# Regrouping value steps and maxima tiles on TensorE in a two-layer hybrid attention kernel

## The reference

```
s = einsum('bqkgd,blkd->bkgql', qblk, k) * scale      # scores
p = softmax(s, axis=-1)                               # over context + latent keys
o = einsum('bkgql,blkd->bqkgd', p, v)                 # value step
```

## Time and profile before

| what | us |
|---|---|
| median of 3 runs | 1099.52 (1099.34 to 1104.13) |
| profiled execution's own time | 1105.77 |
| its span, first to last instruction | 1103.9 |
| PE busy | 969.0 |
| DVE busy | 594.0 |
| attention, first layer | about 255 to 520 |
| attention, last layer | about 811 to 1030 |

### The profile page before, as it was taken

The page is one execution under the profiler, slowest core; times in us unless marked ns, Lnnn a source line. Parts: engine busy times, 40 slices in busy tenths (PEclk is TensorE's granted clock), DMA queues, the critical chain, the costliest instruction groups (busy, mean ns, idle before and its releaser), DMA issues.

```text
span 1103.9 us, 13093 instructions
## 1 busy us (share of the span) xinstructions
PE 969.0 (88%) x4607; PEld 684.6 (62%) x4607; DVE 594.0 (54%) x901; ACT 403.4 (37%) x815; POOL 524.8 (48%) x421
## 2 busy tenths in 40 slices
PE   4799999996899899998995299899968999999793
PEld 2478777985554455555784289789755445555572
DVE  5419230244568499824069548341645758782337
ACT  1521122314354466554200333133434445555320
POOL 2227232352557455553345337243626756566464
PEclk9799999996899899999998689899959989899997
DMA  9756451215232100012431022123142130001421
GB/s 364 270 178 218 157 188 40 77 31 125 55 77 65 34 16 8 16 58 79 169 96 77 38 62 72 58 65 85 49 101 65 37 72 16 15 16 58 160 69 77
DMA packets 44976, 96.91 MB, mean 88 GB/s; under 512 B 9592, under 2 KB 16656, under 8 KB 42864
## 3 DMA queue, kind: packets, MB, share of 16 engines
q1 hardware_dynamic: 43472, 90.83, 26.8%
q10 hardware_dynamic: 1440, 5.24, 1.2%
HBM read 71.33 MB, written 5.26 MB: 69 GB/s over the span
## 4 chain that ended last, share of the span: by engine, by line
PE 71%; DVE 10%; POOL 4%; ACT 4%; SPq 4%; DMA 3%; issue 3%; POOLq 0%; ACTq 0%; DVEq 0%
PE banks L762 13%; PE banks L764 12%; PE banks L763 12%; PE banks L936 11%; PE banks L956 9%; PE banks L914 5%; SPq L588 3%; PE banks L773 2%; DMA area_g<-in_w_ada_dram 2%; DVE negmax L1635 1%; PE banks L975 1%; DVE stats L1515 1%; DVE area_b L1779 1%; PE banks L968 1%; PE banks L826 1%
## 5 line engine op out<-in xcount | busy, mean ns | idle before, releaser
L1393 POOL TENSOR_TENSOR w_split<-w_raw,w_split 128x512 fp32r<-128x512 f32 (+4 forms) x124 | 146.2, 1184 | 258.7 <-ACT w_split L1138 258.6
L762 PE MATMUL banks<-w_split,area_a 128*128 128x512 f32 (+3 forms) x624 | 232.7, 373 | 16.4 <-DVE area_a L1845 9.9
L764 PE MATMUL banks<-w_split,area_a 128*128 128x512 f32 (+3 forms) x624 | 229.8, 368 | 0.0
L763 PE MATMUL banks<-w_split,area_a 128*128 128x512 f32 (+3 forms) x624 | 229.7, 368 | 0.0
L1635 DVE TENSOR_REDUCE negmax<-banks 128x1 f32<-128x768 f32 x160 | 149.6, 951 | 67.3 <-PE banks L914 66.4
L1138 ACT ACTIVATE w_split<-w_raw 128x512 fp32r<-128x512 f32 (+4 forms) x124 | 69.9, 581 | 278.1 <-PE banks L764 278.1
L936 PE MATMUL banks<-area_a 97*128 97x512 f32 (+4 forms) x448 | 135.7, 416 | 17.5 <-DMA area_a<-m_row 11.5
L762 PEld LDWEIGHTS banks<-w_split,area_a 128*128 128x128 f32 x624 | 119.4, 191 | 46.2 <-issue 16.4
L1237 ACT ACTIVATE area_z<-banks 128x512 f32<-128x512 f32 x196 | 109.1, 595 | 103.5 <-PE banks L936 98.2
L764 PEld LDWEIGHTS banks<-w_split,area_a 128*128 128x128 f32 x624 | 118.9, 190 | 16.6
L763 PEld LDWEIGHTS banks<-w_split,area_a 128*128 128x128 f32 x624 | 119.2, 191 | 15.5
(11 more groups left out here) (184 smaller groups left out, 1458.4 us busy)
## 6 DMA issues: line engine op xcount, KB each, us to landing
area_g<-in_w_ada_dram SPq DMA_DIRECT2D x16, 1024.0 KB, 5.8
w_raw<-in_w_in_dram SPq DMA_DIRECT2D x32, 512.0 KB, 3.7
area_g<-in_w_ada_dram SPq DMA_DIRECT2D x16, 512.0 KB, 5.0
w_raw<-in_w_out_dram SPq DMA_DIRECT2D x16, 512.0 KB, 3.9
area_a<-parts SPq DMA_DIRECT2D x72, 96.0 KB
area_a<-parts SPq DMA_DIRECT2D x30, 192.0 KB, 3.6
area_b<-in_x_dram SPq DMA_DIRECT2D x8, 512.0 KB, 9.8
x_mid<-area_b ACTq DMA_DIRECT2D x6, 512.0 KB, 2.7
```

The lines of the kernel that those rows point to most:

```text
L762: nc.tensor.matmul(dst, a[0], b[0], start=first, stop=False)
L763: nc.tensor.matmul(dst, a[0], b[1], start=False, stop=False)
L764: return nc.tensor.matmul(dst, a[1], b[0], start=False, stop=last)
L1393: op = nc.gpsimd.tensor_tensor(lo, raw, hi.bitcast(F32), ALU.subtract)
```

## The change

In each iteration p = 1 to 9 of both layers, two value steps are moved next to each other twice. `mix(L, p, 0)` goes behind tile 1 and `turn_max`, directly ahead of `mix(L, p, 1)`. Tile 4 goes behind `mix(L, p, 3)`, and the second `mla_head` goes ahead of `mix(L, p, 2)`. The lists of the other engines are not touched, and no instruction is added or removed. In iteration 8 and 9 there are no tiles of pair p+2, and in iteration 9 no `turn_max` either.

```
@@ -1042,9 +1042,9 @@
                     max_tile(L, p + 2, 0)
                     turn_denominators(L, p - 1)
                     turn_output(L, p - 1)
-                    mix(L, p, 0)
                     max_tile(L, p + 2, 1)
                     turn_max(L, p + 1)
+                    mix(L, p, 0)
                     mix(L, p, 1)
                     if head_pair(p + 3):
                         mla_head(L, 2 * p + 6)
@@ -1052,11 +1052,11 @@
                     max_tile(L, p + 2, 2)
                     scores(L, p, 5)
                     max_tile(L, p + 2, 3)
-                    mix(L, p, 2)
-                    max_tile(L, p + 2, 4)
                     if head_pair(p + 3):
                         mla_head(L, 2 * p + 7)
+                    mix(L, p, 2)
                     mix(L, p, 3)
+                    max_tile(L, p + 2, 4)
                     max_tile(L, p + 2, 5)
                     if context:
                         scores(L, p, "ctx")
```

## The result

The changed kernel takes 1105.15 us (median of 18 executions, 1103.0 to 1107.3) where the kernel before takes 1101.51 in the same comparison (18 executions, 1098.6 to 1108.5). The ratio is 1.0031, with a 95% interval of 1.0018 to 1.0044: 0.3% slower, where 0.3% faster was forecast. The median lies above the range's upper end, 1103.

A forecast was written before the change was run, and what follows sets the result against it. PE, busy 88% of the span, was taken to bound the kernel. Saving 7.3 us on PE, less 2.0 hidden at pair 4's scores and 1.7 given back, made 3.6: from 1099.52 to 1095.9, forecast 1096, range 1091 to 1103.

The forecast's parts named there:

- Pitches and first edit: PE's list: two adjacent value steps take 1.87 us, the maxima tile behind transposes keeps 0.45; saves 0.15 per iteration.
- no saving at the borders: Rival: the 0.15 and 0.10 at PE's borders move elsewhere in its queue, giving 1100.5 us; chance 0.10.
- Second edit: Tile 4 behind value step 3: PE from tile 3 to the next iteration 3.13 us instead of 3.48, saving 0.35.
- that just fits: Last layer, iteration 1: tile 4's reduction is done at 863.96, before tile 6 wants its banks at 864.20.
- lengthens the wait ... and nothing else: Savings of iterations 2 and 3 only lengthen the wait of pair 4's scores for the maxima row; 2.0 us taken away.
- the clock rival: Additional lower-clock stretches behind longer idle times: two or more, 1102.0 us, chance 0.13; one, 1098.9, chance 0.20.
- The last layer's second mla unit: Iterations 4 to 6: tile 4's reduction starts 0.51 us later, 0.35 isn't gained; 2 x 0.86 = 1.72 given back.
- 0.5 to 0.7 later does no harm there: First layer: DVE's rotation may end 0.5 to 0.7 us later, since ACT reaches that unit only at 399.02.
- The sum: Whole kernel: 7.3 saved on PE, less 2.0 hidden and 1.7 given back, is 3.6 us faster.
- The base: The kernel before was taken at its median of 1099.52 us, from which 3.6 was subtracted.
- The delay's upper bound of 1.0: DVE's delay at the last layer's second mla unit: 0.51 us, bounds 0 and 1.0 (rotation collides longer with POOL).

The follow-up runs named there:

- e18: Unchanged copy of the kernel before, run again to profile its lower group of executions: 1099.32 us.
- The short sum: The changed kernel with POOL's first sum cut to 16 of 512 columns in two iterations of the first layer: 1099.61 us, one execution.
- e7: The kernel before with SP's loads of units 12 and 13 moved behind the maxima row of pair 4: ratio 0.9995.
- e17: Unchanged copy of the kernel before, its third profile, from the upper group: 1105.03 us.
- the filled kernel: The changed kernel with nine thrown-away products on PE ahead of the wait of pair 4's first scores: ratio 0.9990; an unchanged copy measured 1099.45 us.

## Why the prediction was wrong

- **Pitches and first edit: right, the size too small.** The pair takes the 1.87 that was forecast, and the maxima tile behind the transposes, kept at 0.45, has 0.43. The border that the rows didn't show, the transposes ahead of it, saved 0.17 more. The first layer's iteration 1 gained 0.7 (20.4 to 19.7), iterations 6 and 7 0.7 each and iteration 8 0.2, where 0.50 and 0.15 stood. The rival "no saving at the borders" is refuted.
- **Second edit: right at its place,** 3.11 against 3.13. But "that just fits" was wrong for tile 6 in the last layer: it and tile 7 lose 0.3 again, and iteration 1 gained only 0.4 there.
- **"lengthens the wait ... and nothing else", pair 4's scores: this step failed.** The saving did go into the wait, as forecast. But the sum put what comes behind the wait at nothing. With a wait of 2.17 the clock stayed full in the last layer, with 2.83 it fell to 0.66, and the same work took 2.74 us more than in the profile that the prediction was read from. The kernel before has this stretch as well in three of its four profiles, so what the change lost is the chance to escape it, in the last layer and in the first: over iterations 2 and 3 of both layers it takes 1.8 us more than the mean of before, and 3.2 more than e18. Filling the wait wins 2.5 to 4.5 us. This was the clock rival, given 0.13 and 0.20. The argument held against it, that the first layer's wait was long already, was drawn from one profile, of the upper group.
- **The last layer's second mla unit: right.** Tile 4's reduction came late and scores of step 3 moved 0.59 further from tile 3 (13.64 instead of 13.05), forecast 0.51. In the rows below, of DVE and PE after, DVE itself now waits for tile 4 and scores of step 3 still wait 1.55. The waits didn't grow to 2.4, since PE, too, comes later: tiles 6 and 7 wait 0.33 and 0.41, a small wait that wasn't forecast.

```profile
926.19 0.96 DVE L1635 TENSOR_REDUCE negmax<-banks 128x1 f32<-128x768 f32 x1 [0.49 <-PE banks L914]
```

```profile
927.29 0.58 PE L914 MATMUL banks<-area_a 96*128 96x384 f32 x2 [0.33 <-DVE negmax L1635]
...
928.76 0.59 PE L914 MATMUL banks<-area_a 96*128 96x384 f32 x2 [0.41 <-DVE negmax L1635]
...
934.42 0.98 PE L936 MATMUL banks<-area_a 97*128 97x512 f32 x2 [1.55 <-ACT area_z L1237]
```

- **"0.5 to 0.7 later does no harm there", the first layer: this step failed.** The argument followed only the chain through ACT, which has slack. It left out DVE's own list behind the rotation: a reduction, then `mla_low`, which before began 0.59 us ahead of POOL's first sum. After, the sum, which PE's scores release, came 0.73 earlier in the iteration and `mla_low`, held by DVE's list, only 0.13, and each of two iterations lost 1.0 instead of gaining 0.65: 3.3 us. The short sum measured it at 3.4.
- **The sum.** The forecast gain of 3.6, and some 2.0 more at twelve borders that count (0.17 each), less 3.3 of collision, is 2.3 us faster. Measured are 3.6 slower, so 5.9 are open. Iterations 2 and 3 account for 1.8 by the mean of the profiles, and filling gave 2.5 to 4.5 back; the small waits of tiles 6 and 7 are among the rest. The rest stays open: the changed kernel's two profiles are only 1.0 us longer in the mean than the four of before (spans of 1102.8 and 1101.8), so they don't hold the whole of the 3.6, and the stretches differ between executions of one kernel.
- **The base: low by 2.0.** The forecast of 1096 stood on a median of three, 1099.52; over 18 executions the kernel before takes 1101.51. So of the 9.2 us between 1096 and 1105.15, 2.0 are the base and 7.2 the change.
- **The bounds.** The delay's upper bound of 1.0 was for the last layer alone. A bound of the same kind for the first, 1.1 in each of two iterations by a row such as 2.04 beside 0.95, would have put the range's upper end at 1105.

## What to carry to other kernels

When work on the bound engine is packed closer, follow the saving to the next wait and ask what the clock does behind it: in this kernel a wait of 2 to 4 us was followed by up to 3 us more in what came behind it. Taking it away (the row ahead of two loads, 1.0031 to 0.9961) or filling it (1.0031 to 0.9990) brought the changed kernel more than the packing, but it has to be timed: on the kernel before the first of them gained nothing. When a step delays another engine's list, look at every later instruction of that list that stands just ahead of a colliding one, not only at the chain that leads back to the bound engine. And take several profiles of a kernel whose executions lie in two groups before reading a wait as a constant: here the one profile of before that was read first differs from the three others at the very place in question.

## What the runs showed of the hardware

- Four transposes (float32) have a pitch of 0.42 us when a float32r maxima tile follows and 0.59 when a float32 value step does. A border between the two kinds can thus be a gain, where the earlier trace rows has it as a cost of 0.10.
- The same wait, of the same length and at the same place in the work, is followed by the lower clock in one execution and not, or for longer, in another: 2.22 us ahead of 32 transposes, 6.42 us for them in e7 against 3.71 in e18; 2.47 us ahead of tile 4 in the kernel before, with iterations of 21.1, 22.7 and 24.3 us in three of its profiles.
- A low stretch can pay for itself. Where it delayed PE ahead of a DMA that was late anyway, the next stretch didn't come: e18 has 3.2 us less in the first layer than e17.
- A VectorE and a GpSimd operation that start within 0.01 us of each other go either way: VectorE's took 0.95 us in one profile of the filled kernel and 2.09 in the other, with iterations of 25.6 and 26.7 us.
